# Expert 0 pinned to the first expert slot, with its first weight tiles loaded during the scan

## The reference, cut to what matters

```
logits = h @ router                         # (256 tokens, 8 experts)
top_val, top_idx = top_k(logits, 2)
gates = softmax(top_val)
for e in range(8):
    gate, up = split(h @ w_in[e], 2)        # 1024 -> 2 x 3584
    out += (silu(gate) * up) @ w_out[e] * combine[e]    # 3584 -> 1024
```

## Time and profile before

| | us |
|---|---|
| median of 3 runs (lowest, highest) | 1997.37 (1994.3, 1997.76) |
| the profiled execution's own time | 1992.98 |
| its span in the profile | 1991.3 |
| PE busy | 1796.6 (90%) |
| PE weight loads busy | 1415.9 (71%) |
| DVE, ACT busy | 532.7 (27%), 296.0 (15%) |
| DMA, mean over the span | 247 GB/s, 492.54 MB |

### The profile page before, as it was taken

How to read it: one execution, slowest core, us unless ns; L and a number is a source line. 1 busy time by engine, 2 the same in 40 slices (tenths; PEclk the granted TensorE clock), 3 DMA queues, 4 the chain that set the end, 5 groups by cost and what they waited for, 6 DMA issues and landing times. The chain is left out here.

```text
span 1991.3 us, 40332 instructions
## 1 busy us (share of the span) xinstructions
PE 1796.6 (90%) x18321; PEld 1415.9 (71%) x18321; DVE 532.7 (27%) x1222; ACT 296.0 (15%) x639; POOL 71.6 (4%) x109
## 2 busy tenths in 40 slices
PE   5797687889999989988887999999999999999996
PEld 3685576767888867877766444569975898579853
DVE  4434665632000046356654000000000000000002
ACT  2011332210000024323221100000010001010101
POOL 0000321100000000011100000000000000000000
PEclk8899798889999989978887899999999999999999
DMA  9718742203443162100000997999999999999994
GB/s 371 287 44 345 290 171 86 87 10 132 165 150 145 43 236 113 43 8 23 12 7 1 391 389 277 396 427 425 426 413 429 425 426 416 428 426 425 407 428 171
DMA packets 37132, 492.54 MB, mean 247 GB/s; under 512 B 4379, under 2 KB 4540, under 8 KB 7452
## 3 DMA queue, kind: packets, MB, share of 16 engines
q1 hardware_dynamic: 36956, 489.90, 59.9%
HBM read 487.53 MB, written 2.36 MB: 246 GB/s over the span
## 5 line engine op out<-in xcount | busy, mean ns | idle before, releaser
L2064 PE MATMUL bank<-ring,arena 128*32 128x128 f32 x2016 | 227.6, 273 | 0.0
L2061 PE MATMUL bank<-ring,arena 128*32 128x384 f32 x2016 | 224.8, 487 | 2.2 <-DMA ring<-in_experts 2.2
L2064 PEld LDWEIGHTS bank<-ring,arena 128*32 128x32 f32 x2016 | 217.9, 110 | 0.0
L2056 PE MATMUL bank<-ring,arena 128*64 128x256 f32 x1792 | 204.9, 381 | 3.0 <-DMA ring<-in_experts 2.9
L2056 PEld LDWEIGHTS bank<-ring,arena 128*64 128x64 f32 x1792 | 126.5, 137 | 80.4 <-issue 22.7
L2258 DVE TENSOR_TENSOR arena<-bank,arena 128x256 f32<-128x256 f32 (+2 forms) x56 | 28.5, 508 | 547.0 <-PE bank L2064 155.5
L1343 PE MATMUL bank<-arena,ring 128*128 128x256 f32 x704 | 155.3, 382 | 4.0 <-DVE arena L303 3.8
L1343 PEld LDWEIGHTS bank<-arena,ring 128*128 128x128 f32 x704 | 134.0, 191 | 24.5 <-issue 4.1
L2214 ACT ACTIVATE arena<-bank 128x256 f32<-128x256 f32 (+2 forms) x56 | 25.3, 452 | 697.6 <-PE bank L2064 294.0
L1464 PE MATMUL bank<-arena,ring 128*128 128x256 f32 x512 | 115.3, 387 | 4.8 <-DVE arena L303 3.8
L1464 PEld LDWEIGHTS bank<-arena,ring 128*128 128x128 f32 x512 | 98.5, 194 | 23.3 <-issue 6.1
(11 more groups left out here) (391 smaller groups left out, 2246.0 us busy)
## 6 DMA issues: line engine op xcount, KB each, us to landing
ring<-in_experts SPq DMA_DIRECT2D x168, 2048.0 KB, 20.5
ring<-in_stream SPq DMA_DIRECT2D x61, 2048.0 KB, 11.2
xT<-in_xT SPq DMA_DIRECT2D x1, 1024.0 KB, 6.9
arena<-in_s0gd SPq DMA_DIRECT2D x4, 256.0 KB, 3.1
out_sgd<-arena SPq DMA_DIRECT2D x4, 256.0 KB, 2.5
out_y<-arena SPq DMA_DIRECT2D x4, 256.0 KB, 2.5
arena<-in_masks SPq DMA_DIRECT2D x1, 832.0 KB, 4.3
arena<-in_hfw SPq DMA_DIRECT2D x1, 544.0 KB
```

What stands on the lines that cost most here:

```text
L2056: mm = nc.tensor.matmul(out[HALF * x:HALF * x + HALF, 0:256], h[:, j, 0:HALF], w[:, j, 256 * x:256 * x + 256], start=start, stop=stop, til ...
L2061: nc.tensor.matmul(out[lo:hi, 0:3 * P], h[:, j, lo:hi], w[:, j, 0:3 * P], start=start, stop=stop, tile_position=(0, lo), skip_group_check= ...
L2064: mm = nc.tensor.matmul(out[MID:P, r * P:(r + 1) * P], h[:, j, 32 * r:32 * r + 32], w[:, j, 3 * P:4 * P], start=(start and r == 0), stop=s ...
```

## The change

The change has four parts.

1. `key` replaces `tok` in the ranking. It is a copy of the counts with 4096 added to expert 0's, so expert 0 always gets rank 0 and with it slot 0.
2. `feed_first_expert` loads tiles 0 to 6 of expert 0 ahead of the pass: five behind the router's load in the scan block, two in the plan block, when the tiles of the output projection were consumed. `load` in `sp_pass` leaves out those seven in the main pass.
3. The capacities become 96, 96, 128, 64, 96, 64, 96 and 64: four MID, one WIDE and three HALF slots, where there were three MID, one WIDE and four HALF.
4. The pass over the rest moves behind the main pass on all engines, and with it `more` and the branch.

```diff
+        def feed_first_expert(sp, lo, hi):
+
+            for n in range(RING):
+                before = max(m for m in range(STREAM_TILES) if SLOT[m] == n)
+                if lo <= before < hi:
+                    sp.wait_ge(s_used, before + 1)
+                    sp.dma_start(ring[:, n, :], A["experts"][0, n]).then_inc(s_slot[n], 16)
...
                         feed(sp, FIRST["odd_out"])
+                        feed_first_expert(sp, 0, FIRST["odd_out"])
...
-        MAIN_CAPS = [WIDE, HALF] + [MID, HALF] * 3
+        MAIN_CAPS = [MID, MID, WIDE, HALF] + [MID, HALF] * 2
...
                 feed(sp, STREAM_TILES)
+                feed_first_expert(sp, FIRST["odd_out"], STREAM_TILES)
...
-                dve_link(dve, V.tensor_copy(tok, ps[5][:, 0:8]))
-                dve_link.last(dve, V.tensor_tensor(picks[0], rows(tok), tok.unsqueeze(2).broadcast_to([P, NE, NE]), ALU.is_gt))
-                dve_link(dve, V.tensor_tensor(picks[1], rows(tok), tok.unsqueeze(2).broadcast_to([P, NE, NE]), ALU.is_equal))
+                dve_link.last(dve, V.tensor_copy(tok, ps[5][:, 0:8]))
+                dve_link(dve, V.tensor_copy(key, ps[5][:, 0:8]))
+                dve_link(dve, V.tensor_scalar(key[:, 0:1], key[:, 0:1], 4096.0, None, ALU.add))
+                dve_link.last(dve, V.tensor_tensor(picks[0], rows(key), key.unsqueeze(2).broadcast_to([P, NE, NE]), ALU.is_gt))
+                dve_link(dve, V.tensor_tensor(picks[1], rows(key), key.unsqueeze(2).broadcast_to([P, NE, NE]), ALU.is_equal))
...
-                if n >= RING or m.at:
+                if n < RING and m.at:
+                    return
+                if n >= RING:
                     sp.wait_ge(m.used, m.base + p - RING + 1)
...
             @block.vector
             def _(dve):
                 V = nc.vector
                 dve.wait_ge(s_plan, PLAN_READY)
+                dve_pass(dve, main)
+                dve.wait_ge(main.acc, main.base + 4 * NE)
                 with dve.If(more(dve) > 0):
                     dve_pass(dve, rest)
                     dve.wait_ge(rest.acc, rest.base + 4 * NE)
-                dve_pass(dve, main)
-                dve.wait_ge(main.acc, main.base + 4 * NE)
```

More of the change, by code:

```diff
@@ L1845, in program @@
         caps = take(NE)
+        key = take(NE)
         most = take(2)
@@ L2285, in _ @@
                 sp.wait_ge(s_plan, ORDER_KNOWN)
+                sp_pass(sp, main)
                 with sp.If(more(sp) > 0):
+                    main.consumed(sp, 3 * STEPS - 1)
                     sp_pass(sp, rest)
-                    rest.consumed(sp, 3 * STEPS - 1)
-                sp_pass(sp, main)
                 for b in range(4):
@@ L2300, in _ @@
             def _(act):
+                act_pass(act, main)
                 with act.If(more(act) > 0):
+                    act.wait_ge(main.acc, main.base + 4 * NE)
                     act_pass(act, rest)
                     act.wait_ge(rest.acc, rest.base + 4 * NE)
-                act_pass(act, main)
                 n4.act_squares(act, 13)
@@ L2309, in _ @@
             def _(pe):
+                pe_pass(pe, main)
                 with pe.If(more(pe) > 0):
+                    pe.wait_ge(main.acc, main.base + 4 * NE)
                     pe_pass(pe, rest)
                     pe.wait_ge(rest.acc, rest.base + 4 * NE)
-                pe_pass(pe, main)
                 n4.pe(pe, ps[0])
```

## The result

The changed kernel took 2031.12 us, median of 4 runs (2027.97 to 2031.23), beside 1996.64 us for the kernel before, measured in turn with it (4 runs, 1994.3 to 1997.76). The ratio is 1.017, 95% interval 1.0153 to 1.0188: 34.5 us slower, where 33.6 were forecast.

The account below looks back on a forecast made before the run. PE's own work was taken to bound the expert block; 39.0 - 3.0 - 3.3 - 0.7 + 1.6 + 0 = +33.6 us on the 1997.4 median gave 2031.0, forecast as 2030 us, range 2019 to 2040.

Parts of the forecast that it names:

- What bounds the block: Expert block: PE's own work sets its time, transfers are level some microseconds behind; PE waited 8.9 us for weights.
- Capacities, +39.0: Expert block: one HALF slot becomes MID, adding 39.0 us of PE work over seven steps, with nothing covering it.
- Waits, -3.0: Expert block: with 161 tiles instead of 168, PE's waits for weights fall from 8.9 to 6 us.
- The start, -4.0: Before the first expert product: flag load and branch leave the front, -3.3 us; first two gathers with 96 columns, -0.7.
- The tail, +1.6: After the last accumulation: DVE's flag and branch cost 1.6 us, PE's branch just hides; ends 0 and +5.
- The scan, 0: Scan and out projection: the seven early tiles make nothing wait, 0 us; ends -1 and +5.
- the transfers decide: Rival, expert block: the shorter list of transfers ends it, 34.6 us saved, 1960 us in all; chance 0.05.
- it cancels: Rival, whole kernel: vanished waits and the start offset a MID slot costing some 15 us; 1995 to 2000; chance 0.03.
- The disturbed scan and the dear tail: Rival, scan and tail: +5 us each, full waits, no gain at the start; 2046 us; chance 0.06.
- the span from PE's first product to the end of its last scatter: Sign, expert block: it grows by 33 to 39 us, otherwise the forecast is wrong.

Follow-up runs that it names:

- experiment 6: Kernel before with half of every expert tile not loaded: by columns 1984.4 us, ratio 0.995; by partitions 2038.31 us in the profiled execution.
- experiment 1: Kernel before with only the new capacities and the pinned expert 0, no early tiles, rest's pass still first: 2026.05 us, ratio 1.0151.
- experiment 4: Changed kernel without the early tiles, all 168 loaded in the pass: 2023.13 us, ratio 1.014.
- experiment 3: Kernel before with only the pass over the rest, its flag and branch moved behind the main pass: 1990.17 us, ratio 0.9981.
- experiment 2: Changed kernel with slot 0 back at 64 tokens: 1992.56 us, ratio 0.999.
- experiment 5: Changed kernel again, 2032.71 us; with two of its five scan tiles left in the scan, 2028.12; with all in the plan block, 2028.12.
- experiment 7: Kernel before with only its last slot at 96 instead of 64 tokens: 2026.74 us, ratio 1.0173.

## Why the prediction was right, point by point

*What bounds the block.* Right. That PE's waits and not the busy shares decide is shown by experiment 6: without half the traffic the block lost 10.2 us, where the waits were 8.9. By the rule that the weight loads' share should be read instead of the matmuls' (the Trainium skill, "Trainium Kernel Development and Optimization", Best Practices) the transfers would have been the bound, and this measurement speaks against it: the HALF slots, with the weight loads busy for 51.4 of 86.6 us, had nothing to gain from less traffic but the waits.

*Capacities, +39.0.* Right in kind, 3 us too high. In the profiles the block without waits grew from 852.8 to 890.9, 38.1; of these some 2.1 are the first products, which ran 4.3 us at a granted clock of 0.50 where it was 1.00 before. So PE's added work is 36.0. The step of the working that was too high is that one HALF slot becomes MID and all else stays. The order changed too, and with it what stands ahead of a slot. A MID slot without a slot before it has no scatter, and behind a MID one it costs less than behind a HALF one; the WIDE slot, first before, now has a scatter to do. The starts of steps in slot 0 and in the WIDE slot:

```profile
1124.00 0.48 PE bank L2088 x3
...
1140.34 0.48 PE bank L2088 x3
...
1368.82 0.44 PE bank L2088 x4
...
1390.72 0.44 PE bank L2088 x4
```

So a step is 16.34 us in slot 0, 17.20 in slot 1 (1242.09 to 1259.29) and 21.90 in the WIDE slot, where it was 21.04. One such step of each of the eight slots adds up to 125.4 us against 120.1 before: 5.3 a step instead of 5.66, 1.5 us less over four. The slots' first steps add 4.9 instead of 5.5, and the HALF slots that stayed came out 0.8 shorter without their waits. That is 2.9 of the 3.0.

*Waits, -3.0.* The size was nearly right (-3.8), the reason was not. I had them fall as the transfers got shorter. With the new capacities they are 5.1 us with 161 tiles to load (the changed kernel) and 4.8 and 4.9 with 168 (experiments 1 and 4): the number of tiles does not matter. They sit in the last HALF slot, where each step takes 11.7 us of work and 14.8 of transfer (6.0 us there before, 5.1 after). The others, 3 us before, stood around the ends of two earlier HALF slots; after the change there are none of these. Since experiment 1 has them gone with 168 tiles, it is the new order of slots that removes them; that this is because the block now begins with three slots whose steps are longer than their transfers is argued and not shown.

*The start, -4.0.* Measured -4.6. PE's late start was its branch, as taken from the 3453 ns: moved alone (experiment 3) it gives 3.8. The two gathers did not get shorter with 96 columns, 3.74 us against 3.80; with ACT's copies (0.50 against 0.61) the way to the first product lost 0.25 of the 0.7 us. The two more instructions cost 0.3 as taken: 79.4 us in experiment 1 against 79.0. About 0.8 us more appears in the four kernels with tiles in the scan (73.9 to 74.4 against 75.2 in experiment 4), and no row explains it.

*The tail, +1.6.* The mechanism was right, the size was 4.4. DVE's flag and branch took 1.53 us and PE's branch, 3.87 us, was hidden, more amply than the working had it: PE's sequencer read the flag at 2003.3 and branched at 2004.2, while the scatter that began at 2003.24 was still running, and not behind it. The rest is the clock: scatter and norm took 5.78 and 6.29 us against 3.70 and 5.43, at granted clocks of 0.63 and 0.58 against 1.00 and 0.69. This part comes and goes: the last scatter took 3.70 us in experiments 2 and 4, 4.75 in 3, 5.10 in 1. What moves the fall of the clock from run to run stays open. That a jump to code not yet held has to be fetched (the Trainium skill, "Runtime: NRT & Kernel Launch", Instruction fetch mechanics) is what PE shows again; DVE's branch took 73 ns and 0.53 us of issue, so the price was not paid on every engine.

*The scan, 0.* Wrong: +2.7 in the profile, 3 to 6 us in the three profiles with five tiles, inside the ends given (-1 to +5) but for one. I had looked for a wait on a transfer and found none; there is none after the change either. The tiles landed at 882.05, 5 us later than worked out, and still ahead of the store at 898.30. What the term left out is PE's own instruction fetches beside the tiles, and the clock, as experiment 5 has it.

*The rivals.* That the transfers decide fell with experiments 4 and 6, that it cancels with 1 and 7. The disturbed scan and the dear tail were both there in part, 2.7 and 2.8 us, and were balanced in part by the other terms: capacities came to 38.1 with the low clock in them instead of 39.0, waits to -3.8 instead of -3.0, the start to -4.6 instead of -4.0. The profiles' stretches add up to 36.8 us and the medians differ by 34.5. So the forecast of 33.6 is right by its large term; that it came within 1 us is luck. Of the signs given, the span from PE's first product to the end of its last scatter grew from 866.7 to 903.1, by 36.4 us, inside the 33 to 39.

## What to carry to other kernels

Where two resources look full, ask what each would give back if the other were free: here less traffic gave back 10 us. A free PE could give back some 30 at most, by an estimate from these rows (168 tiles x 4.95 us = 832 of 862 us), while one larger slot added 36 to PE's work. Loading early helps only if the consumer waits for the load at that place; here the first product waited for a gather, and the change came with a larger slot in the engine that was the bound. When slots of different sizes are moved, price each one by what stands ahead of it. A branch over a long stretch of code is cheap where the engine has slack, and a flag can be read long before it is needed. Transfers that nobody waits for may still delay others on the same DMA engines, an engine's instructions among them, as the fetches beside the five tiles suggest: look at the instruction queue too.

## What was not expected of the hardware

- Half of a tile by partitions (64 of 128) came at 206 GB/s with a DMA share of 1.01, where the whole came at 423, so it took the same time; half by columns ran at 212 to 215 GB/s with a DMA share of 0.63.
- In that same run with 64 partitions PE stood still for 29.0 us in the MID slots. Each of the 15 stops ended 2.7 to 3.1 us after an instruction fetch began. That PE waited for its instructions is read off these times and not tested.
- Five tiles of 2 MB in flight lengthened a scan that waits for none of them by 3 to 6 us. The instruction fetch beside them began some 3 us late and PE stopped for 0.4 to 1.8 us; the later part, in pairs that ran after the tiles had landed (44.7 us a pair against 44.3), goes with the moment at which the granted clock falls. What moves that moment is open.
